# Gated units' projections as three products of rounded parts, split by ACT, DVE and POOL and added back by POOL

## The reference

```
h = rms_norm(x) * (1 + scale1) + shift1
u = h @ w_in
conv_in = u[..., :1024]               # 512 values, 512 gates
q, k, v = u[..., 1024:2560]           # 8 heads of 64
gates   = sigmoid(u[..., 2560:])
v_conv  = val * sigmoid(gate)         # gated units, val and gate = halves of conv_in
v_conv  = depthwise conv, width 31, over v_conv
```

## Time and profile before

| | |
|---|---|
| median of 3 runs | 2795.89 us (2795.61 to 2797.86) |
| the profiled execution | 2797.56 us, its span 2795.8 us |
| busy: PE, DVE, ACT, POOL | 2676.0, 1697.2, 1257.6, 193.0 us |
| mean granted clock of PE | 0.982 |

### The profile page before, as it was taken

The page is one execution under the profiler, slowest core; times in us unless marked ns, Lnnn a source line. Parts: engine busy times, 40 slices in busy tenths (PEclk is TensorE's granted clock), DMA queues, the critical chain, the costliest instruction groups (busy, mean ns, idle before and its releaser), DMA issues.

```text
span 2795.8 us, 49220 instructions
## 1 busy us (share of the span) xinstructions
PE 2676.0 (96%) x21611; PEld 2005.2 (72%) x21611; DVE 1697.2 (61%) x2007; ACT 1257.6 (45%) x1795; POOL 193.0 (7%) x180
## 2 busy tenths in 40 slices
PE   6999999999999999959999999999999999999994
PEld 3555577666666698747887787778777877887783
DVE  3699234677223244466767677676767766676664
ACT  4000134555112132245656565655555555555554
POOL 0000001110000000010110111011101110110000
PEclk9999999999999999969999999999999999999997
DMA  8232222001233372267988898798888988898884
GB/s 259 90 90 76 61 56 50 15 14 33 73 85 90 91 219 106 98 222 258 295 273 272 285 291 280 267 298 276 283 270 293 288 271 283 282 296 261 283 279 168
DMA packets 457503, 543.73 MB, mean 194 GB/s; under 512 B 26304, under 2 KB 409387, under 8 KB 457290
## 3 DMA queue, kind: packets, MB, share of 16 engines
q1 hardware_dynamic: 449610, 519.60, 57.2%
q0 software_dynamic: 7680, 20.98, 3.4%
HBM read 513.27 MB, written 27.28 MB: 193 GB/s over the span
## 4 chain that ended last, share of the span: by engine, by line
PE 89%; DVE 5%; DMA 2%; ACT 2%; issue 1%; SPq 0%; POOL 0%; DVEq 0%; POOLq 0%; ACTq 0%
PE bank L652 85%; PE bank L655 5%; DVE arena L1649 2%; DVE arena L1722 1%; DMA arena<-in_w_attn_o 1%; DVE arena L1732 1%; ACT arena L1269 0%; DVE arena L2050 0%; DMA arena<-in_x_sample 0%; DVE w_down L1766 0%; DMA arena<-in_w_in 0%; DMA arena<-xhat,arena 0%; ACT arena L1273 0%; SPq L465 0%; ACT w_up L1320 0%
## 5 line engine op out<-in xcount | busy, mean ns | idle before, releaser
L652 PE MATMUL bank<-arena 128*64 128x128 f32 (+8 forms) x3716 | 734.2, 408 | 19.9 <-ACT arena L1269 5.1
L1980 DVE TENSOR_TENSOR slot_lo<-slot,e_hi 128x2048 fp32r<-128x2048 f32 x256 | 579.2, 2289 | 166.2 <-ACT e_hi L1462 162.5
L652 PEld LDWEIGHTS bank<-arena 128*128 128x128 f32 (+3 forms) x3716 | 431.3, 165 | 287.0 <-issue 217.3
L1462 ACT ACTIVATE e_hi<-slot 128x2048 fp32r<-128x2048 f32 x256 | 481.5, 1917 | 0.0
L652 PE MATMUL bank<-e_hi,xe_hi 128*128 128x512 f32 x1024 | 418.2, 408 | 0.0
L652 PE MATMUL bank<-e_hi,xe_lo 128*128 128x512 f32 x1024 | 404.8, 395 | 0.0
L652 PE MATMUL bank<-slot_lo,xe_hi 128*128 128x512 f32 x1024 | 400.4, 391 | 0.0
L652 PE MATMUL bank<-slot,arena 128*32 128x128 f32 (+1 forms) x10240 | 363.6, 297 | 6.0 <-DVE arena L1990 3.5
L652 PEld LDWEIGHTS bank<-slot,arena 128*32 128x32 f32 x10240 | 285.3, 111 | 72.4 <-issue 34.0
L1984 DVE TENSOR_TENSOR slot_lo<-slot,e_hi 128x2048 fp32r<-128x2048 f32 x128 | 288.8, 2287 | 77.9 <-ACT e_hi L1464 77.9
L655 PE MATMUL bank<-arena 128*128 128x128 f32 (+3 forms) x1415 | 203.9, 277 | 53.7 <-DVE arena L1578 12.2
(11 more groups left out here) (221 smaller groups left out, 2541.0 us busy)
## 6 DMA issues: line engine op xcount, KB each, us to landing
slot<-in_w_gate_e SPq DMA_DIRECT2D x128, 1024.0 KB, 5.6
slot<-in_w_up_e SPq DMA_DIRECT2D x128, 1024.0 KB, 9.1
slot<-in_w_down_e SPq DMA_DIRECT2D x128, 1024.0 KB, 6.9
arena<-in_w_in SPq DMA_DIRECT2D x68, 512.0 KB, 5.1
arena<-in_w_ada SPq DMA_DIRECT2D x48, 512.0 KB, 4.9
arena<-in_w_conv_pw SPq DMA_DIRECT2D x24, 256.0 KB, 5.7
arena<-in_w_attn_o SPq DMA_DIRECT2D x24, 256.0 KB, 5.3
yacc<-arena SPq DMA_DIRECT2D x10, 512.0 KB, 2.6
```

Source lines behind the costliest of these rows:

```text
L652: return nc.tensor.matmul(out, lhsT, rhs, start=start, stop=stop)
L1462: A_(halves(e_hi[c % 2])[:, :, rows4, :], halves(slot[q])[:, :, rows4, :], ACT.Copy).then_inc(ehi_ok, 1)
L1980: V_.tensor_tensor(halves(slot_lo[q])[:, :, rows4, :], halves(slot[q])[:, :, rows4, :], halves(e_hi[c % 2])[:, :, rows4, :].bitcast(F32), ...
```

## The change

In the first half each float32 product becomes three products of rounded parts, as in the later stages. ACT rounds the tokens (`g_hi`, into `g_up`, in the raw tokens' place) and the weights (`gw_hi`, into `gw_up`, in the queries' place). The low parts take the place of what was split: of the tokens in `hT` by DVE (`g_lo`), of the weights in `ws` by DVE for tile 0 (`gw_lo`) and by POOL for tiles 1 to 3. As the second half and later stages want the float32 tokens, POOL adds high and low back into `hT`, 8 sums for each token tile, once PE is through with the tile; the first query tile waits for these sums one by one, and ACT, before it copies a query or key, for all 24. The semaphore `res9` gives way to `pool_sum`, and the counts that the merge stage waits for are raised by what is now counted before. The order of taps and gated units on DVE stays.

```diff
...
         h_down = [rounded_at(f"h_down{q}", HT + 2 * T * q, 2, T) for q in range(KD // 2)]
+        g_up = [rounded_at(f"g_up{c}", K + T * c, 1, T) for c in range(KD)]
+        g_down = [h_down[c // 2][:, c % 2, :] for c in range(KD)]
+        gw_up = [rounded_at(f"gw_up{i}", Q + 2048 * i, KD, 256) for i in range(2)]
+        gw_down = [rounded_at(f"gw_down{i}", R + 2048 * i, KD, 256) for i in range(2)]
...
-        rinv6, router, res9 = sem("rinv6"), sem("router"), sem("res9")
+        rinv6, router, pool_sum = sem("rinv6"), sem("router"), sem("pool_sum")
...
             nc.gpsimd.memset(glu, 0.0).then_inc(pads, 1)
+            pool.wait_ge(wl_ok, 2)
+            for j in range(1, 4):
+                for half in range(2):
+                    pool.wait_ge(wh_ok, 2 * j + half + 1)
+                    ks = slice(4 * half, 4 * half + 4)
+                    nc.gpsimd.tensor_tensor(gw_down[j % 2][:, ks, :], ws[j % 2][:, ks, :], gw_up[j % 2][:, ks, :].bitcast(F32),
+                                            ALU.subtract).then_inc(wl_ok, 1)
+            for tc, (t0, n) in enumerate(TOK):
+                pool.wait_ge(u_ready, 18 + 2 * tc + 2)
+                for c in range(KD):
+                    nc.gpsimd.tensor_tensor(hT[:, c, t0:t0 + n], g_up[c][:, 0, t0:t0 + n].bitcast(F32),
+                                            g_down[c][:, t0:t0 + n].bitcast(F32), ALU.add).then_inc(pool_sum, 1)
             pool.wait_ge(conv_done, 1)
             def bias_rows(hp, h):
...
-            nc.gpsimd.tensor_tensor(mt6[:, 0:2, :], mt6[:, 0:2, :], g1row[:, 4:6, :], ALU.mult).then_inc(res9, 1)
-            pool.wait_ge(res9, 1)
+            nc.gpsimd.tensor_tensor(mt6[:, 0:2, :], mt6[:, 0:2, :], g1row[:, 4:6, :], ALU.mult).then_inc(pool_sum, 1)
+            pool.wait_ge(pool_sum, 24 + 1)
-            nc.gpsimd.tensor_tensor(mt6[:, 2:4, :], mt6[:, 2:4, :], g1row[:, 6:8, :], ALU.mult).then_inc(res9, 1)
-            pool.wait_ge(res9, 2)
+            nc.gpsimd.tensor_tensor(mt6[:, 2:4, :], mt6[:, 2:4, :], g1row[:, 6:8, :], ALU.mult).then_inc(pool_sum, 1)
+            pool.wait_ge(pool_sum, 24 + 2)
...
                     pe.wait_ge(u_free, 15)
                 for i in range(0, 2):
                     for jj in range(2):
+                        j = 2 * i + jj
                         pe.wait_ge(ws_in[jj], i * 32 + (64 + 64 * half))
                         for tc, (t0, n) in enumerate(TOK):
                             pe.wait_ge(qk_free if half else u_free, i * 6 + (3 * jj + tc + 1))
                             for h in range(2):
+                                out, cols = bank[2 * tc + h][:, 0:n], slice(P * h, P * h + P)
                                 for k in range(KD):
-                                    if half == i == jj == h == 0:
-                                        pe.wait_ge(h_dve if k % 2 else h_act, 4 * tc + k // 2 + 1)
-                                    last = mm(bank[2 * tc + h][:, 0:n], ws[jj][:, k, P * h:P * h + P], hT[:, k, t0:t0 + n],
-                                              k == 0, k == KD - 1)
+                                    if half:
+                                        if j == h == 0:
+                                            pe.wait_ge(pool_sum, 8 * tc + k + 1)
+                                        last = mm(out, ws[jj][:, k, cols], hT[:, k, t0:t0 + n], k == 0, k == KD - 1)
+                                    else:
+                                        if tc == h == 0 and k % 4 == 0:
+                                            pe.wait_ge(wl_ok, 2 * j + k // 4 + 1)
+                                        if j == h == 0:
+                                            pe.wait_ge(hl_ok, 8 * tc + k + 1)
+                                        mm(out, gw_up[jj][:, k, cols], g_up[k][:, 0, t0:t0 + n], k == 0, False)
+                                        mm(out, gw_up[jj][:, k, cols], g_down[k][:, t0:t0 + n], False, False)
+                                        last = mm(out, gw_down[jj][:, k, cols], g_up[k][:, 0, t0:t0 + n], False, k == KD - 1)
                                 last.then_inc(u_ready, 1)
                             if tc:
                                 ada_turn(5 + tc, i * 4 + (8 * half + 2 * jj + tc + 8))
...
-                        pe.wait_ge(wl_ok, i * 2 + (8 * tc + s + 1))
-                        pe.wait_ge(hl_ok, 4 * (tc + 1))
+                        pe.wait_ge(wl_ok, 8 + i * 2 + (8 * tc + s + 1))
+                        pe.wait_ge(hl_ok, 24 + 4 * (tc + 1))
                         for which in range(2):
                             out = bank[4 * s + which][:, 0:n]
                             for k in range(KD):
...
             act.wait_ge(t1_act, 12)
-            for g, (c, tc) in enumerate(tile_groups()):
-                if g % 2 == 0:
-                    t0, n = TOK[tc]
-                    cnd = 1 if tc == 2 else 0
-                    if tc == 0:
-                        act.wait_ge(mod1_ok, c // 4 + 1)
-                    A_(hT[:, c, t0:t0 + n], hT[:, c, t0:t0 + n], ACT.Identity, bias=sh1[:, c, cnd:cnd + 1],
-                       scale=A1[:, c, cnd:cnd + 1]).then_inc(h_act, 1)
+            def affine(tc, c):
+                t0, n = TOK[tc]
+                cnd = 1 if tc == 2 else 0
+                if tc == 0:
+                    act.wait_ge(mod1_ok, c // 4 + 1)
+                A_(hT[:, c, t0:t0 + n], hT[:, c, t0:t0 + n], ACT.Identity, bias=sh1[:, c, cnd:cnd + 1],
+                   scale=A1[:, c, cnd:cnd + 1]).then_inc(h_act, 1)
+            def g_hi(tc, cs_):
+                t0, n = TOK[tc]
+                for c in cs_:
+                    act.wait_ge(h_dve if c % 2 else h_act, 4 * tc + c // 2 + 1)
+                    A_(g_up[c][:, 0, t0:t0 + n], hT[:, c, t0:t0 + n], ACT.Copy).then_inc(hh_ok, 1)
+            def gw_hi(j, half):
+                act.wait_ge(ws_in[j % 2], 64 + 32 * (j // 2))
+                ks = slice(4 * half, 4 * half + 4)
+                A_(gw_up[j % 2][:, ks, :], ws[j % 2][:, ks, :], ACT.Copy).then_inc(wh_ok, 1)
+            act.wait_ge(t1_ready, 24)
+            affine(0, 0)
+            affine(0, 2)
+            g_hi(0, range(0, 4))
+            gw_hi(0, 0)
+            affine(0, 4)
+            affine(0, 6)
+            g_hi(0, (4, 5))
+            gw_hi(0, 1)
+            g_hi(0, (6, 7))
+            for tc in (1, 2):
+                for c in range(0, KD, 2):
+                    affine(tc, c)
+                g_hi(tc, range(KD))
+            gw_hi(1, 0)
+            gw_hi(1, 1)
             for i in range(0, 2):
...
                         act.wait_ge(u_free, i * 6 + (m + 2))
                         A_(sg[:, m % 2, 0:n], bank[2 * tc + 1][:, 0:n], ACT.Sigmoid).then_inc(sg_ok, 1)
                         ada_steps(tc, i * 4 + (2 * jj + 8), i * 8 + (16 + 4 * jj))
+                        if tc == 0 and 1 <= 2 * i + jj <= 2:
+                            for part in range(2):
+                                gw_hi(2 * i + jj + 1, part)
+            act.wait_ge(pool_sum, 24)
             for i in range(0, 2):
                 for jj in range(2):
                     for tc, (t0, n) in enumerate(TOK):
...
             affine(0, (5, 7))
-            affine(1, (1, 3, 5, 7))
-            affine(2, (1, 3, 5, 7))
+            def g_lo(tc, cs_):
+                t0, n = TOK[tc]
+                for c in cs_:
+                    dve.wait_ge(hh_ok, 8 * tc + c + 1)
+                    V_.tensor_tensor(g_down[c][:, t0:t0 + n], hT[:, c, t0:t0 + n], g_up[c][:, 0, t0:t0 + n].bitcast(F32),
+                                     ALU.subtract).then_inc(hl_ok, 1)
+            def gw_lo(half):
+                dve.wait_ge(wh_ok, half + 1)
+                ks = slice(4 * half, 4 * half + 4)
+                V_.tensor_tensor(gw_down[0][:, ks, :], ws[0][:, ks, :], gw_up[0][:, ks, :].bitcast(F32), ALU.subtract).then_inc(wl_ok, 1)
+            g_lo(0, range(0, 4))
+            gw_lo(0)
+            g_lo(0, (4, 5))
+            gw_lo(1)
+            g_lo(0, (6, 7))
+            for tc in (1, 2):
+                affine(tc, (1, 3, 5, 7))
+                g_lo(tc, range(KD))
             def leave(dst, tc_, Ac, Bc, ready, done):
...
             def weight_lo(s, tiles):
-                dve.wait_ge(wh_ok, tiles)
+                dve.wait_ge(wh_ok, 8 + tiles)
                 src, dst = (wm_first, w_down_first) if tiles == 1 else (wm[s], w_down[s])
                 V_.tensor_tensor(dst, src[:, 0:16, :], w_up[s].bitcast(F32), ALU.subtract).then_inc(wl_ok, 1)
...
             def h_lo(tc):
                 t0, n = TOK[tc]
                 for q in range(KD // 2):
-                    dve.wait_ge(hh_ok, 4 * tc + q + 1)
+                    dve.wait_ge(hh_ok, 24 + 4 * tc + q + 1)
                     V_.tensor_tensor(h_down[q][:, :, t0:t0 + n], hT[:, 2 * q:2 * q + 2, t0:t0 + n],
                                      h_up[q][:, :, 0:n].bitcast(F32), ALU.subtract).then_inc(hl_ok, 1)
             h_lo(0)
```

## The result

The changed kernel took 2818.35 us (median of 4 runs, 2816.75 to 2820.71), the one before 2796.88 (2795.61 to 2800.65): the ratio is 1.0075, 95% interval 1.0058 to 1.0093, so 21.5 us slower. The profiled execution has a span of 2815.9 us, 20.1 more than before.

What follows compares the result with a forecast made beforehand. The last gated unit on DVE, which lets PE's queries' products start, was taken to bound the kernel. -4.5 - 1.4 + 33.1 + 1.9 = +29.1 us on 2795.89 gave 2825 us, range 2791 to 2836.

Steps and rivals of the forecast that it cites:

- PE's 28 us: Rounded products spare PE 7.0 us per weight tile, 28.0 over four; only 5.9 reach the last gated unit. All arriving: 0.01.
- The start: PE's first product waits for affines, roundings and a subtraction on ACT and DVE: +2.5 us.
- The cover: ACT's remaining token work at the start stays hidden behind PE, thinly; otherwise the second token tile starts 1 to 2 us late.
- The 1.42 us wait: DVE's one idle time, before the gated unit at 158.14, goes because PE is ahead: -1.4 us.
- The clock: After a wait of 20 us or more before the queries' products, PE restarts at a low clock: +1.9 us.
- POOL beside the taps: POOL's subtractions and sums hold DVE's taps back for their full length, 35.6 us less 2.5 beside gated units: +33.1 us.
- no interference: Rival: POOL doesn't hold DVE's taps back; -4.0 us in sum, so 2792 us; chance 0.24.
- POOL starved: Rival: DVE's taps always win, POOL's sums end late and PE waits until near 299; some 2885 us; chance 0.03.
- Interference in part: Rival: POOL costs DVE's taps a third to a half of 33.1, +7 to +13 us, so 2803 to 2809; chance 0.12.

Runs made afterwards that it cites:

- e5: Changed kernel with POOL's work kept and the gated units moved earlier in DVE's order: 2781.05 us, 0.9941 of the kernel before.
- e6: As e4, with the gated units also earlier in DVE's order, where PE's new pace delivers them: 2775.01 us, 0.9919 of the kernel before.
- e7: Kernel before the change (float32 products), with gated units earlier in DVE's order, where its PE delivers them: 2798.23 us, ratio 1.0000.
- e3: Changed kernel with all of POOL's new operations made equal-sized clears that read nothing; some low parts are zero: 2793.76 us, 0.9987 of the kernel before.
- e2: Changed kernel with POOL's sums made copies of the high part (one input stream), POOL's subtractions kept: 2804.69 us, one run.
- e4: Changed kernel with POOL's new work done by DVE, order of taps and gated units kept: 2808.66 us, 1.0042 of the kernel before.
- e8: Changed kernel with each of POOL's 512-column sums done as two of 256: 2811.9 us, 1.0051 of the kernel before.

## Why the prediction was right

Forecast 2825, measured 2818.35, slower as forecast and for the forecast reason.

- **PE's 28 us don't arrive.** Right: PE's wait went from 1.0 to 42.6 us, and e5, e6 and e7 show that it is the place of the last gated unit that keeps them. The 28 were too many by 2.4, though: from its first product to its wait PE took 152.3 us before (51.53 to 203.8) and 126.7 in the changed kernel (53.37 to 222.65, less the wait of 42.6), 25.6 less. Behind DVE this costs nothing; in e6 it shows. So a tile is spared 6.4 us and not 7.0. About half of the gap is the pace: PE's timeline of the changed kernel has 38 starts from 69.88 to 78.70, 0.232 us each and not the 0.229 of the earlier trace rows, 0.3 us over the 96 products of a tile. The rest is open.
- **The start**: forecast +2.5, measured +1.8. That the taps began just the 4.5 us earlier that the sum had is luck: the start slipped by 0.7 us less and tile 0 was spared about as much less, and the two cancel. The cover held: no second wait for tokens.
- **The 1.42 us wait** is gone, as forecast.
- **The clock**: forecast +1.9, measured +2.8; the low clock lasted past 226, longer than the start's rows had suggested. The same 540 products lost 2.5, 2.6, 2.7 and 2.1 us behind waits of 18.8 (e3), 29.9 (e2), 33.0 (e4) and 36.5 us (e8), so the loss does not grow with such a wait; behind 6.9 us (e5) it was 1.5.
- **POOL beside the taps** is the term that was mis-sized: 33.1 us forecast, 17.8 + 4.5 + 1.4 = 23.7 measured. (Against e3, the same kernel without POOL's reads, it is 222.18 - 199.01 = 23.2.) The step that failed is "each POOL operation holds a tap back for as long as it runs". The delays measured are 2.0, 0.9 and 0.34 us where POOL alone takes 2.36, 1.27 and 0.73 (the middle one measured, the outer two worked out from other sizes; the two half tiles at 68.83 took 2.38 each with no tap beside them): each time about 0.37 us less. Over 28 operations that is 10.4 us. The term was off by only 9.4, as less than forecast stayed hidden beside gated units: 4 x 2.0 + 16 x 0.9 + 8 x 0.34 = 25.1 less 23.7 leaves 1.4 us, not 2.5. e8 shows that the free part belongs to the operation, not to the column.
- The rivals: no interference was run as e3 (2794 against 2792), POOL starved never occurred (POOL got one turn at each tap; its price was also summed wrong, as the 4 us taken off were already in the 289: some 2892, not 2885). Interference in part can be told apart only by size: +7 to +13 was forecast for it, +21.5 measured. From 256 to 512 and to 1024 columns the delay grows by 2.2 ns a column, near POOL's own pace of 2.1, which fits one engine standing still while the other reads, all but the fixed part. How the reads of the two follow each other inside an operation no trace shows.

The rule of the Trainium skill weighed in the prediction (SBUF — State Buffer, "Who interferes with whom") was right in kind: two inputs against a reader contend (taps 2.51 us), a writer doesn't disturb (e3), and an instruction with one input in SBUF and one in PSUM isn't held back (681 ns). "For the whole instruction" is 0.37 us too much here.

## What to carry to other kernels

Before handing elementwise work to POOL, look at what DVE does beside it: where DVE's instructions read two operands from SBUF, a POOL operation that reads two cost DVE its own length less a small fixed part here, and for additions of 512 columns this was more (0.9 us) than DVE's own time for them (0.61); at 256 columns it was even. And when an engine is made faster in a stage where another follows an order written out by hand, move the hand-over points in the same change: here the same rounded products were 21.5 us slower with the old order and 17 to 23 us faster with a new one.

## What had not been expected of the hardware

The first tap of a block (L1726 in the changed kernel, a multiply-add by two scalars of one SBUF operand, 1310 columns) takes 0.96 us alone, less than the 1.58 of the others, and 1.36 beside POOL's sums of 256 columns (212.34 in the changed kernel, 204.65 in e8). One operand in SBUF is then no protection. The Trainium skill (SBUF — State Buffer, "Who interferes with whom") says that such an instruction can run in a mode that also takes the port pair shared with GpSimd, and then contends; the two durations agree. In e3 it took 0.96 again, with no clear beside it at that moment, so its behaviour beside a pure writer stays open. And neither engine starved the other: POOL's sums and DVE's taps took turns one by one over the whole stretch, about 2.5 us a pair at 512 columns and 1.96 at 256.
